# One RWKV-7 / gated-MLP layer in split fp32: the high weight part streams both activation halves in one 512-column matmul in three stages, and VectorE adds the halves

## The reference

```python
def merge_branches(p, y_rwkv, ...):
    y_gmlp = chunk_mlp(p[..., RWKV_COLS:OFF_GATES], ln_v_g, ln_v_b, w_spatial, b_spatial)
    gate_a, gate_b = jnp.split(p[..., OFF_GATES:], 2, axis=-1)      # p = h @ w_in
    m = jax.nn.sigmoid(gate_a) * (y_rwkv @ w_proj_a) + jax.nn.sigmoid(gate_b) * (y_gmlp @ w_proj_b)
    return m @ w_out

def conv_glu_ffn(h, w_up, conv_w, w_down, grid):
    up = dwconv2d_grid(h @ w_up, conv_w)
    a, b = jnp.split(up, 2, axis=-1)
    return (jax.nn.silu(a) * b) @ w_down

mix = merge_branches(...);  x = x + gt1 * rmsnorm(mix, g_post1)
h2 = rmsnorm(x, g_pre2) * (1.0 + sc2) + sh2
x = x + gt2 * rmsnorm(conv_glu_ffn(h2, w_up, conv_ffn, w_down), g_post2)
```

## Time and profile before

| | |
|---|---|
| runs | median 3150.03 us of 3 (3148.62, 3150.03, 3157.80) |
| the profiled execution's own time | 3148.07 us |
| its span, first to last instruction | 3146.3 us |
| mean granted TensorE clock | 0.971 of full |
| PE busy | 2962.2 us (94%) |
| DVE busy | 1744.2 us (55%) |
| ACT busy | 951.9 us (30%) |

### The profile page before, as it was taken

How to read it: one execution, slowest core, us unless ns; L and a number is a source line. 1 busy time by engine, 2 the same in 40 slices (tenths; PEclk the granted TensorE clock), 3 DMA queues, 4 the chain that set the end, 5 groups by cost and what they waited for, 6 DMA issues and landing times.

```text
span 3146.3 us, 70342 instructions
## 1 busy us (share of the span) xinstructions
PE 2962.2 (94%) x28320; PEld 2232.4 (71%) x28320; DVE 1744.2 (55%) x3292; ACT 951.9 (30%) x1635; POOL 436.0 (14%) x580
## 2 busy tenths in 40 slices
PE   5899999999999999999998899999989999999997
PEld 1345555555555555555555579999979999999997
DVE  1136555565455655556555354444358988886434
ACT  1122222222222222222222143333354444443333
POOL 0001110111101111011111020000003333331000
PEclk8899999999999999999999999999989999999999
DMA  8512222122121221212212254455434545554553
GB/s 330 234 72 100 88 75 88 57 99 93 70 88 62 94 90 73 88 62 95 88 48 97 108 208 159 177 185 187 161 134 174 185 176 185 184 177 162 180 174 137
DMA packets 66076, 412.32 MB, mean 131 GB/s; under 512 B 8176, under 2 KB 10864, under 8 KB 25328
## 3 DMA queue, kind: packets, MB, share of 16 engines
q1 hardware_dynamic: 65136, 407.51, 36.1%
q0 software_dynamic: 768, 2.10, 0.2%
HBM read 405.38 MB, written 4.19 MB: 130 GB/s over the span
## 4 chain that ended last, share of the span: by engine, by line
PE 85%; DVE 6%; DMA 3%; issue 3%; ACT 2%; POOL 0%; SPq 0%; ACTq 0%; DVEq 0%; POOLq 0%; PEldq 0%
PE PB L651 18%; PE Q L899 6%; PE Q L900 6%; PE Q L904 6%; PE PB L899 4%; PE PB L900 4%; PE PB L904 4%; PE CH L904 3%; PE CH L900 3%; PE CH L899 3%; DMA ring<-w_mod_dram 3%; PE Q L784 3%; PE PB L636 2%; PE Q L767 2%; PE CH L583 2%
## 5 line engine op out<-in xcount | busy, mean ns | idle before, releaser
L651 PE MATMUL PB<-hT,ring 128*128 128x512 f32 (+1 forms) x1536 | 687.9, 557 | 5.4 <-PEq L640 5.4
L1585 DVE TENSOR_TENSOR w_lo_r<-ring,w_hi_r 128x1536 fp32r<-128x1536 f32 (+3 forms) x178 | 387.6, 2177 | 270.3 <-ACT w_hi_r L1194 270.3
L1194 ACT ACTIVATE w_hi_r<-ring 128x2048 fp32r<-128x2048 f32 (+2 forms) x178 | 325.8, 1830 | 453.9 <-PE Q L904 211.8
L651 PEld LDWEIGHTS PB<-hT,ring 128*128 128x128 f32 x1536 | 252.4, 189 | 140.6 <-issue 96.9
L900 PE MATMUL PB<-hT_r,w_hi_r 128*128 128x256 f32 x832 | 204.5, 285 | 0.0
L1745 DVE TENSOR_TENSOR w_lo_r<-ring,w_hi_r 128x1408 fp32r<-128x1408 f32 x62 | 101.2, 1633 | 147.9 <-ACT w_hi_r L1308 147.9
L899 PE MATMUL PB<-hT_r,w_hi_r 128*128 128x256 f32 x704 | 175.7, 289 | 4.7 <-DVE hT_r L1672 4.7
L899 PE MATMUL Q<-ff_hi_r,w_hi_r 128*128 128x256 f32 x704 | 175.6, 288 | 1.8 <-ACT w_hi_r L1308 1.8
L900 PE MATMUL Q<-ff_lo_r,w_hi_r 128*128 128x256 f32 x704 | 172.9, 284 | 0.0
L899 PE MATMUL CH<-hT_r,w_hi_r 128*128 128x256 f32 x704 | 170.9, 283 | 0.0
L900 PE MATMUL CH<-hT_r,w_hi_r 128*128 128x256 f32 x704 | 170.9, 283 | 0.0
(11 more groups left out here) (262 smaller groups left out, 5991.0 us busy)
## 6 DMA issues: line engine op xcount, KB each, us to landing
ring<-w_mod_dram SPq DMA_DIRECT2D x96, 1024.0 KB, 5.2
ring<-w_up_dram SPq DMA_DIRECT2D x88, 1024.0 KB, 4.8
ring<-w_rkv_dram SPq DMA_DIRECT2D x48, 1024.0 KB, 4.8
ring<-w_down_dram SPq DMA_DIRECT2D x64, 704.0 KB, 4.0
ring<-w_ga_dram SPq DMA_DIRECT2D x16, 1024.0 KB, 4.8
ring<-w_gb_dram SPq DMA_DIRECT2D x16, 1024.0 KB, 4.7
ring<-w_pa_dram SPq DMA_DIRECT2D x16, 1024.0 KB, 4.8
ring<-w_out_dram SPq DMA_DIRECT2D x16, 1024.0 KB, 4.8
```

Of the source, the lines that this page charges most:

```text
L651: last = mm(PB[slot % 2][:, 0:cols], tile(n, kt), hT[:, kt, 0:cols], start=(kt == 0), stop=(kt == KT - 1))
L1194: f(w_hi_r[:, r % 2, 0:n], ring[:, r, 0:n], ACT.Copy).then_inc(hi_rdy, 1)
L1585: tt(w_lo_r[:, r, 0:n], ring[:, r, 0:n], as_f32(w_hi_r[:, r % 2, 0:n]), ALU.subtract).then_inc(lo_rdy, 1)
```

## The change

In `merge`, `out` and `down` the two matmuls of the high weight become one of 512 columns (`high_pair`). The low and high activation of a contraction tile are streamed together, so the bank's two halves hold high weight by high activation and high weight by low activation. The low-weight pass is as before and adds to the half of the high activation. VectorE then adds the two halves (`halves`, a tensor_reduce) out of PSUM, and ScalarE's sigmoid and squares read the sum from SBUF; its copies are gone. For the two gates ScalarE puts a copy of `h_hi_r` beside `h_lo_r` during `gu`. `gu` and `up` stay as they were.

```diff
+            def high_pair(bank, r, k, both, start):
+                mm(bank[:, :], w_hi_r[:, r % 2, k * P:(k + 1) * P], both, start=start, stop=False)
 ...
+            pe.wait_ge(hr_rdy, 4)
 ...
                     for kt in range(n):
-                        with_high(Q[r][:, 0:T], r, kt, hi[:, kt], lo[:, kt], kt == 0)
+                        high_pair(Q[r], r, kt, both[kt], kt == 0)
                     low_ready("merge", i, r)
                     for kt in range(n):
-                        last = with_low(Q[r][:, 0:T], r, kt, hi[:, kt], kt == n - 1)
+                        last = with_low(Q[r][:, half * T:(half + 1) * T], r, kt, hi[:, kt], kt == n - 1)
 ...
-                    pe.wait_ge(o_sb, i * 4 + r + 1)
+                    pe.wait_ge(o_sum, i * 4 + r + 1)
                     for kt in range(KT):
-                        with_high(four[r][:, 0:T], r, kt, m_hi_r[:, kt], m_lo_r[:, kt], kt == 0)
+                        high_pair(four[r], r, kt, m_r[:, :, kt], kt == 0)
 ...
-                            with_high(Q[2 + q][:, 0:T], r, k, ff_hi_r[:, kt], ff_lo_r[:, kt], kt == 0)
+                            high_pair(Q[2 + q], r, k, ff_r[:, :, kt], kt == 0)
 ... ScalarE
+                    if i == 1:
+                        act.wait_ge(hl_rdy, 1)
+                        f(h_in_r[:, 4 * r:4 * r + 4], as_f32(h_hi_r[:, 4 * r:4 * r + 4]), ACT.Copy).then_inc(hr_rdy, 1)
 ...
-                        product(r, "merge", 0, i, 1)
-                        f((sga, sgb)[r], Q[r][:, 0:T], ACT.Sigmoid).then_inc(me_act, 1)
+                        act.wait_ge(me_sum, i * 2 + r + 3)
+                        f((sga, sgb)[r], (sga, sgb)[r], ACT.Sigmoid).then_inc(me_act, 1)
 ...
-                    product(r, "out", 0, i, 1)
+                    act.wait_ge(o_sum, i * 4 + r + 5)
                     to = bass.ds(i * 4 + r, 1)
-                    f(mixT[:, to, :].rearrange("p a b -> p (a b)"), four[r][:, 0:T], ACT.Copy)
-                    f(sq[:, to, :].rearrange("p a b -> p (a b)"), four[r][:, 0:T], ACT.Square).then_inc(o_sb, 1)
+                    f(sq[:, to, :].rearrange("p a b -> p (a b)"), mixT[:, to, :].rearrange("p a b -> p (a b)"),
+                      ACT.Square).then_inc(o_sb, 1)
 ... VectorE
+            def halves(out, bank):
+                return nc.vector.tensor_reduce(out, bank[:, :].rearrange("p (a b) -> p b a", a=2), mybir.AxisListType.X, ALU.add)
 ...
                     lows("merge", i, r, KT, "out")
-                    if r >= 2:
+                    product(r, "merge", 0, i, 1)
+                    if r < 2:
+                        halves((sga, sgb)[r], Q[r]).then_inc(me_sum, 1)
+                    else:
                         o, g = ((mta, sga), (mtb, sgb))[r - 2]
-                        product(r, "merge", 0, i, 1)
-                        dve.wait_ge(me_act, i * 2 + r + 1)
-                        m = V.tick(tt(o, g, Q[r][:, 0:T], ALU.mult))
+                        flow(halves(o, Q[r]))
+                        dve.wait_ge(me_act, i * 2 + r - 1)
+                        m = V.tick(tt(o, o, g, ALU.mult))
 ...
             for r in range(4):
                 lows("out", 3, r, 4, "up")
+                out_sum(3, r)
 ...
+            def down_sum(i, q):
+                product(3, "down", q, i, 2)
+                halves(mixT[:, bass.ds(i * 2 + q, 1), :].rearrange("p a b -> p (a b)"), Q[2 + q]).then_inc(dn_sum, 1)
```

More of the change, by code:

```diff
@@ L219, in layer_kernel @@
         w_lo_r = rounded("w_lo_r", at_ring, 0, 4, REG)
[L220 to L223, removed]
+        yg_r = rounded("yg_r", at_arena, 0, 2, GG, T)
+        yg_hi_r, yg_lo_r = yg_r[:, 0], yg_r[:, 1]
+        m_r = rounded("m_r", at_arena, FFA, 2, KT, T)
+        m_hi_r, m_lo_r = m_r[:, 0], m_r[:, 1]
         h_hi_r = rounded("h_hi_r", at_arena, FFA + 2 * KT * T, KT, T)
[L225 to L228, removed]
+        yr_r = rounded("yr_r", at_arena, FFA + 3 * KT * T, 2, KT, T)
+        yr_lo_r, yr_hi_r = yr_r[:, 0], yr_r[:, 1]
+        ff_r = rounded("ff_r", at_arena, FFA, 2, FT, T)
+        ff_hi_r, ff_lo_r = ff_r[:, 0], ff_r[:, 1]
         hT_r = rounded("hT_r", at_hT, 0, KT, TT)
         h_lo_r = hT_r[:, :, T:TT]
+        h_in_r = hT_r[:, :, 0:T]
         h2_lo_r, h2_hi_r = hT_r[:, :, 0:T], hT_r[:, :, T:TT]
@@ L331, in layer_kernel @@
         gs_ps = sem("gmlp_spatial_done")
+        hr_rdy = sem("h_high_in_place")
         gu_act = sem("gmlp_u_gelu_done")
         yg_rdy = sem("gmlp_out_ready")
+        me_sum = sem("merge_gate_halves_added")
         me_act = sem("merge_gates_ready")
         m_rdy = sem("merged_ready")
+        o_sum = sem("w_out_halves_added")
         o_sb = sem("w_out_copied")
@@ L341, in layer_kernel @@
         ff_rdy = sem("ff_ready")
+        dn_sum = sem("down_halves_added")
         dn_sb = sem("down_copied")
@@ L931, in _ @@
             pe.wait_ge(yg_rdy, GG + 2)
-            pe.sem_inc(me_act, 2)
+            pe.wait_ge(hr_rdy, 4)
+            pe.sem_inc(me_sum, 2)
             pe.sem_inc(m_rdy, 1)
@@ L942, in _ @@
                     if r < 2:
-                        pe.wait_ge(me_act, i * 2 + r + 1)
+                        pe.wait_ge(me_sum, i * 2 + r + 1)
                     else:
                         pe.wait_ge(m_rdy, i + 1)
-                    hi, lo, n = ((h_hi_r, h_lo_r, KT), (h_hi_r, h_lo_r, KT), (yr_hi_r, yr_lo_r, KT), (yg_hi_r, yg_lo_r, GG))[r]
+                    n = GG if r == 3 else KT
+                    if r < 2:
+                        both, hi, half = [hT_r[:, kt] for kt in range(n)], h_hi_r, 0
+                    else:
+                        pair, hi, half = ((yr_r, yr_hi_r, 1), (yg_r, yg_hi_r, 0))[r - 2]
+                        both = [pair[:, :, kt] for kt in range(n)]
                     for kt in range(n):
-                        with_high(Q[r][:, 0:T], r, kt, hi[:, kt], lo[:, kt], kt == 0)
+                        high_pair(Q[r], r, kt, both[kt], kt == 0)
                     low_ready("merge", i, r)
                     for kt in range(n):
-                        last = with_low(Q[r][:, 0:T], r, kt, hi[:, kt], kt == n - 1)
+                        last = with_low(Q[r][:, half * T:(half + 1) * T], r, kt, hi[:, kt], kt == n - 1)
                     last.then_inc(used[r], 1)
             pe.wait_ge(m_rdy, KT + 1)
+            pe.sem_inc(o_sum, 4)
             pe.sem_inc(o_sb, 4)
@@ L1007, in _ @@
                 up_four(i, False)
+            pe.sem_inc(dn_sum, 2)
             pe.sem_inc(dn_sb, 2)
@@ L1012, in down_two @@
                 for q in range(2):
-                    pe.wait_ge(dn_sb, i * 2 + q + 1)
+                    pe.wait_ge(dn_sum, i * 2 + q + 1)
                     for r in range(4):
@@ L1308, in down_one @@
                         f(w_hi_r[:, r % 2, 0:FT // 4 * P], ring[:, to, 0:FT // 4 * P], ACT.Copy).then_inc(hi_rdy, 1)
-                product(3, "down", q, i, 2)
-                f(mixT[:, bass.ds(i * 2 + q, 1), :].rearrange("p a b -> p (a b)"), Q[2 + q][:, 0:T], ACT.Copy)
-                f(sqd[q], Q[2 + q][:, 0:T], ACT.Square).then_inc(dn_sb, 1)
+                act.wait_ge(dn_sum, i * 2 + q + 3)
+                f(sqd[q], mixT[:, bass.ds(i * 2 + q, 1), :].rearrange("p a b -> p (a b)"), ACT.Square).then_inc(dn_sb, 1)
             with act.Fori(0, KT // 2 - 1) as i:
@@ L1639, in _ @@
             with dve.Fori(0, KT - 1) as i:
-                V.enter(i, 2)
+                V.enter(i, 4)
                 merge_four(i)
@@ L1643, in _, with out_sum @@
             merge_four(KT - 1)
+            def out_sum(i, r):
+                product(r, "out", 0, i, 1)
+                halves(mixT[:, bass.ds(i * 4 + r, 1), :].rearrange("p a b -> p (a b)"), four[r]).then_inc(o_sum, 1)
             with dve.Fori(0, 3) as i:
@@ L1646, in _ @@
                     low("out", i, r + 2)
+                    out_sum(i, r)
             for r in range(4):
                 lows("out", 3, r, 4, "up")
+                out_sum(3, r)
             def normed_residual(n, gain, at, out, done):
@@ L1749, in _ @@
                     low_down(i, k)
+                    if k % 4 == 3:
+                        down_sum(i, k // 4)
             for k in range(6):
                 low_down(KT // 2 - 1, k)
+                if k == 3:
+                    down_sum(KT // 2 - 1, 0)
+            down_sum(KT // 2 - 1, 1)
             normed_residual(4, 3, 5 * KT, x_out, out_rdy)
```

## The result

The changed kernel takes 3129.59 us, median of 7 runs (3125.3 to 3140.05), against 3150.03 before: the ratio is 0.994, with a 95% interval of 0.9921 to 0.9958. The time lies inside the stated range, but the gain, 20.4 us, is half of the 40 us forecast. It lies inside only because the range had been drawn wide enough to take in rival B: the forecast's own bounds ended at some 3116 us.

What follows compares the result with a forecast made beforehand. The PE's matmuls were taken to bound the stages, 0.120 us apart, waiting for weight loads. 3148.07 - 44.5 (wide matmuls) + 4.3 (ends) = 3107.9 us; the median lies 2.0 higher, so 3110; range 3101 to 3134.

Steps and rivals of the forecast that it cites:

- rival B: Merged matmuls: each matmul pays the 0.013 us whatever its length; 512 columns take 0.227, gain 24.7 us, time 3130; 13 in 100.
- What bounds the stages: `merge`, `out`, `down`: the PE never waits, so time is the number of matmuls by 0.12 us between starts.
- the reading of the 0.013 us: High-weight pairs: 256 columns wait for their weights, 512 would not; 0.216 for 0.240 us, 1856 pairs, gain 44.5 us.
- The sums: VectorE's 96 tensor_reduces in `merge`, `out`, `down`: 0.68 us each, 1.2 as the bad end; hidden in `merge` and `down`.
- The wait in `out`: PE's `add_square` behind the previous product's square: chain 5.29 us against a 5.73 us product, slack 0.44, nothing lost.
- The three ends: Not hidden: `merge` to `out` 1.5 us, `out` to the norm 2.3, end of `down` 0.5; together 4.3 us lost.
- The copies of `h_hi_r`, the DMA: Four ScalarE copies before `merge`, free with over 1 us of cover; weights every 5.4 us for 5.8, also free.
- Rivals C and D: Merged matmuls: C, slow streaming, 512 columns take 0.240, time 3154, 13 in 100; D, loads in the open, 3303, 4 in 100.

Runs made afterwards that it cites:

- `micro_rows`: Kernel computing nothing of the layer, only rows of matmuls, each of one kind, on a quiet chip: fp32r starts 0.2267 us apart at 512 columns, 0.1198 at 256.

## Why the prediction was half right

**What bounds the stages: right.** The PE's row of matmuls sets the time before and after. The delays that the change brought inside the stages are small, 0.5 us in `out` and 0.26 in `down`.

**The step that failed** is the reading of the 0.013 us beyond the 0.107 of streaming: "I read this as a matmul of 256 columns waiting for its weights", and with it "I take half of the f32 record's 0.43, 0.216". I took it that a wide matmul has room for the load and so sheds the 0.013. The runs show that each fp32r matmul of 128 weight columns pays 0.0133 whatever its width from 256 to 512. A pair saves one such addition and not both: 0.240 less 0.2267 is 0.0133, not 0.024. That is rival B as it was written, 24.7 us by its own sum and 3130 us, for which I gave 13 in 100. Two of my rows misled. Two-column f32 loads stand 0.113 apart, near 0.120 but not at it: the rows of 192 and 128 columns show a floor of 0.111 of that kind, and 256 columns stand above it. What exactly makes the 0.0133, and whether the load has a share in it at 256 columns, stays open. And the f32 record's 0.43 less 0.427 of streaming is true of f32, where the addition is 0.0025, and says nothing of fp32r. The load and the matmul start in lockstep in rows 2 either way, since a load starts with the matmul before it in both readings.

**From 24.7 to 21.35.** By stage rival B's sum is 11.9, 3.4 and 9.4 us; measured were 10.9, 2.9 and 7.6. The irregular starts behind a change between widths cost 0.019 us for each change there and back, by the rows of `micro_rows`; with 64, 16 and 64 of them that is 1.2, 0.3 and 1.2, 2.7 in all. That accounts for `merge`. In `out` the waits took 0.5 us, and a shorter stretch at the lower clock (granted 0.50 for 3.8 us in place of 5.3) gave about as much back. At that clock itself nothing was to be gained: a wide matmul stood at 0.427, two narrow ones at 2 x 0.213. `down` is still 0.6 us short, 0.26 of it in its one wait (2.04 for 1.78 us). I did not take the rest apart.

**The sums: right.** 0.68 us each by the row (680 to 692 ns, all 96), hidden in `merge` and `down`, and in `out` but for 0.5 us:

```profile
L1618 DVE TENSOR_REDUCE arena<-Q x64: 680/683/685, 1900.7 to 2207.5; 128x256 f32<-128x512 f32 x64
L1618 DVE TENSOR_REDUCE hT<-Q x16: 683/684/692, 2871.0 to 3104.0; 128x512 f32 x14, 128x256 f32<-128x512 f32 x2
```

**The wait in `out`: right for all products but the first that meets it.** A product takes 5.99 us (5.73 forecast, with the 0.216) where it took 6.17. (The prediction's 6.11 divides its window by 14 products; the window's 695 records, 50 a product, make 13.9.) The square then ends 0.5 us ahead of L975, and ScalarE's `high` is due later than the square:

```profile
2227.90 0.42 ACT L1274 ACTIVATE arena<-hT  x1 [3.16 <-DVE hT L1618]
2229.05 1.92 ACT L1212 ACTIVATE w_hi_r<-ring 128x2048 fp32r<-128x2048 f32 x1 [0.73 <-PE CH L909]
```

One product earlier it was not in time. L975 started 0.31 us behind the matmul ahead of it, where it starts 0.12 behind elsewhere:

```profile
2222.28 0.42 ACT L1274 ACTIVATE arena<-hT  x1 [3.16 <-DVE hT L1618]
2222.75 0.30 PEld L975 LDWEIGHTS Q<-arena,ones 128*128 128x128 f32 x2 [0.23 <-ACT arena L1274]
```

Two later products start 0.17 and 0.20 us late behind L975 and make up part of it; what they wait for I did not read. All three delays stand in both traces of the changed kernel, and none in the version without the sums or in the one with the sums first; together they are the 0.5 us of `out`.

**The three ends: right,** 1.36, 2.29 and 0.49 us for 1.5, 2.3 and 0.5. The end of `out` in the changed kernel, which answers to the earlier trace rows:

```profile
2309.17 1.76 DVE L1605 TENSOR_TENSOR w_lo_r<-ring,w_hi_r 128x1536 fp32r<-128x1536 f32 x1 [3.63 <-ACT w_hi_r L1212]
...
2310.85 0.68 DVE L1618 TENSOR_REDUCE hT<-CH 128x256 f32<-128x512 f32 x1
...
2311.57 0.42 ACT L1274 ACTIVATE arena<-hT 128x256 f32<-128x256 f32 x1 [2.43 <-DVE hT L1618]
```

**The copies of `h_hi_r`, the DMA: right.** No wait for a weight's DMA stands in the stages. From `gu` to `merge` it is 56.6 us for 56.2, but not by the copies: `gu` has 0.5 us more at one wait of the PE for VectorE, whose multiplication (L1638) took 0.95 us there in place of 0.43, and that is ahead of the first copy. `gu` is 50.3 us long in all five traces with the change and 49.8 in the two without; the cause stays open.

**Rivals C and D** are out: 512 columns take 0.2267 and not 0.240, and no load was paid in the open.

By these runs the rule of the Trainium skill (TensorE: Matmul & The Clock Gate, Back-to-back issue gap: columns at 2.4 GHz plus about 2.5 ns) fits bf16 and each plain f32 record here, the latter counted at two clocks a column, and misses fp32r by 11 ns a matmul.

## What to carry to other kernels

A distance between matmuls that exceeds their streaming has to be priced in the same dtype and at two widths before one says which part of it goes away; a row of another dtype is no substitute, and a dozen lines of matmuls on an idle chip settle it. Merging two matmuls of one weight removes one fixed addition, here 0.0133 us of 0.240; it pays as long as the work that it moves to another engine is hidden, and its price shows at the ends of the stages, where that work stands in a chain. Put what the PE waits for ahead of what it needs later: with the sums before the splits the version here gained 6.8 us more, and the kernel before had 3.6 us to gain from its own order.

## What the hardware showed that was not expected

- At a granted clock of 1.00, fp32r matmuls with 128 weight columns stand at their columns over 2.4 GHz plus 0.0133 us for 256, 320, 384 and 512 columns; bf16 and plain f32 records at plus 0.0025. With 64 or 32 weight columns, 256 streamed columns take 0.113 us but 384 still 0.173. With 128 weight columns and 192 or 128 streamed the distance is 0.111 both times.
- Behind a change of width from 256 to 512 the first five starts are 0.228 to 0.236 us apart before they settle at 0.227, on an idle chip and in `merge` alike (medians there 0.233, 0.236, 0.228, 0.232, 0.231).
- Weights that repeat are no cheaper than weights that change: 0.2273 against 0.2267 us with 512 columns.
- A tensor_reduce that adds the two halves of a PSUM bank takes 0.683 us, no more than the tensor_scalar that reads 512 columns of PSUM in the earlier trace rows (0.681), in spite of its two pieces 256 columns apart.
